# An RWKV scan on one core: the operands for the chunk ends dropped, and the order on the engines rewritten

## The reference, cut to the stage that is changed

The whole reference is three blocks; the change lies in the mixer below. `B` is 1, `L` is 512, and the 1024 channels are 16 heads of `N` = 64.

## Time and profile before

| | |
|---|---|
| time, median of three runs | 4066.91 us (4065.96 to 4070.18) |
| time of the profiled execution | 4058.67 us |
| its span, first to last instruction | 4057.3 us |
| stretch of the scan, first mask of the first half to first mask of the last | 1777.39 to 2128.79 us |
| in that stretch: TensorE, VectorE, ScalarE busy | 292.56, 286.25, 160.38 us of 351.40 |
| mean granted TensorE clock in it | 0.94 |

### The profile page before, as it was taken

One profiled execution on the slowest core, in us unless ns is written; L12 is line 12 of the kernel. 1 busy time (PEld: TensorE's weight loads), 2 busy tenths in 40 slices (PEclk: granted clock), 3 DMA queues, 4 the chain that ended last, 5 costly groups with the idle time before them and its releaser, 6 DMA issues. The chain is left out here.

```text
span 4057.3 us, 63395 instructions
## 1 busy us (share of the span) xinstructions
PE 3854.9 (95%) x26412; PEld 3044.2 (75%) x26412; DVE 2282.2 (56%) x3290; ACT 1318.3 (32%) x2121; POOL 1348.0 (33%) x550
## 2 busy tenths in 40 slices
PE   8999999999999999988888999999999999999998
PEld 6856788876778887577775788777777787877886
DVE  5746477567677665568884776465550626251033
ACT  3246233343223332444443433322222112103222
POOL 1001444443234441000001444355554343654442
PEclk9999999999999999999998999999999999999998
DMA  5310222232112223441112222222122112222221
GB/s 176 125 50 35 93 94 99 88 132 104 62 63 104 103 83 111 160 151 45 49 45 87 83 89 98 90 83 83 67 79 75 66 63 90 88 104 83 101 86 62
DMA packets 43375, 359.85 MB, mean 89 GB/s; under 512 B 4307, under 2 KB 4691, under 8 KB 23804
## 3 DMA queue, kind: packets, MB, share of 16 engines
q1 hardware_dynamic: 43132, 356.35, 24.3%
HBM read 333.79 MB, written 22.28 MB: 88 GB/s over the span
## 5 line engine op out<-in xcount | busy, mean ns | idle before, releaser
L352 POOL TENSOR_TENSOR ffn_weights_low<-weight_ring,ffn_weights_high 128x2048 fp32r<-128x2048 f32 x128 | 591.8, 4624 | 787.3 <-ACT ffn_weights_high L451 786.6
L202 PE MATMUL banks<-ffn_in_high,ffn_weights_low 128*128 128x512 f32 x2048 | 800.8, 391 | 12.8 <-POOL ffn_weights_low L352 8.8
L203 PE MATMUL banks<-ffn_in_low,ffn_weights_high 128*128 128x512 f32 x2048 | 798.2, 390 | 0.0
L204 PE MATMUL banks<-ffn_in_high,ffn_weights_high 128*128 128x512 f32 x2048 | 798.2, 390 | 0.0
L202 PEld LDWEIGHTS banks<-ffn_in_high,ffn_weights_low 128*128 128x128 f32 x2048 | 385.4, 188 | 98.9 <-POOL ffn_weights_low L352 11.3
L204 PEld LDWEIGHTS banks<-ffn_in_high,ffn_weights_high 128*128 128x128 f32 x2048 | 385.3, 188 | 80.6
L203 PEld LDWEIGHTS banks<-ffn_in_low,ffn_weights_high 128*128 128x128 f32 x2048 | 385.3, 188 | 80.0 <-issue 0.7
L451 ACT ACTIVATE ffn_weights_high<-weight_ring 128x2048 fp32r<-128x2048 f32 x128 | 245.2, 1915 | 560.0 <-PE banks L204 560.0
L605 DVE SCALAR_TENSOR_TENSOR ffn_gate<-ffn_up,columns_sb,ffn_gate 128x511 f32<-128x511 f32 (+1 forms) x132 | 273.6, 2072 | 160.8 <-ACT ffn_value L495 160.8
L3764 POOL TENSOR_TENSOR third_weights_low<-weight_ring,third_weights_high 128x1024 fp32r<-128x1024 f32 x144 | 359.8, 2498 | 11.5
L3762 POOL CAST third_weights_high<-weight_ring 128x1024 fp32r<-128x1024 f32 x144 | 159.4, 1107 | 512.4 <-PE banks L204 483.4
(11 more groups left out here) (646 smaller groups left out, 7474.4 us busy)
## 6 DMA issues: line engine op xcount, KB each, us to landing
weight_ring<-weights SPq DMA_DIRECT2D x144, 2048.0 KB, 7.7
scan_in<-rwkv_operands SPq DMA_DIRECT2D x7, 1280.0 KB, 5.8
rwkv_operands<-rwin_staged SPq DMA_DIRECT2D x23, 256.0 KB, 3.3
scan_in<-rwkv_operands SPq DMA_DIRECT2D x8, 512.0 KB, 3.9
bias_tiles<-bias_rows SPq DMA_DIRECT2D x8, 448.0 KB, 8.9
residual<-x SPq DMA_DIRECT2D x4, 512.0 KB, 7.1
hyena_u_x_T<-decay SPq DMA_DIRECT2D x2, 1024.0 KB, 8.0
rwkv_residual<-residual SPq DMA_DIRECT2D x1, 2048.0 KB, 7.2
```

The source lines that it names most:

```text
L202: pe.matmul(out, w[1], x[0], start=start, stop=False, skip_group_check=True)
L203: pe.matmul(out, w[0], x[1], start=False, stop=False, skip_group_check=True)
L204: return pe.matmul(out, w[0], x[0], start=False, stop=stop, skip_group_check=True)
L352: pool.tensor_tensor(parts[1], landed, parts[0].bitcast(F32), ALU.subtract).then_inc(S["split"], 1)
```

```diff
             def offsets(u):
...
-                for p in range(2):
-                    need(u, "phi_done", p + 1)
-                    act.activation(psi[:, p::2, :], B(d, 2 + p)[:, 256:512].rearrange("p (j k) -> p j k", j=JT), ACT.Copy)\
+                need(u, "sums_read", 1)
+                for c in (*order[d][1 - d::2], *order[d][d::2]):
+                    need(u, "phi_sum", 2)
+                    at = 256 + c // 2 * RW_N
+                    act.activation(psi[:, c, :], B(d, 2 + c % 2)[:, at:at + RW_N], ACT.Copy, scale=pe_end[:, u % 4, c:c + 1])\
                        .then_inc(S["psi_done"], 1)
...
-            def tails(u):
-                if not 0 <= u < HALVES:
-                    return
-                behind = upto(left) if u % 2 == FWD else ahead(grown)
-                dve.tensor_tensor(by_chunk(hat[:, 0, :]), by_chunk(k), behind, ALU.mult)
-                dve.tensor_tensor(by_chunk(hat[:, 1, :]), by_chunk(b), behind, ALU.mult).then_inc(S["tails_ready"], 1)
...
-                need(u, "diag_done", 1)
+                need(u, "psi_done", N_CHUNKS)
                 for p in range(2):
-                    need(u, "phi_sum", p + 1)
-                    dve.tensor_tensor(phi[:, p::2, :], B(d, 2 + p)[:, 0:256].rearrange("p (j k) -> p j k", j=JT), diag[:, d, p::2, :], ALU.add)\
+                    dve.tensor_tensor(phi[:, p::2, :], B(d, 2 + p)[:, 0:256].rearrange("p (j k) -> p j k", j=JT), spread(eye, JT), ALU.add)\
                        .then_inc(S["phi_done"], 1)
...
-                dve.tensor_tensor(state[:, d, n + 1, :], B(d, 3)[:, n * RW_N:(n + 1) * RW_N], psi[:, order[d][n], :], ALU.add)\
-                   .then_inc(S["state_done"], 1)
+                c = order[d][n]
+                dve.scalar_tensor_tensor(out=state[:, d, n + 1, :], in0=B(d, 3)[:, n * RW_N:(n + 1) * RW_N], scalar=pe_end[:, u % 4, c:c + 1],
+                                         in1=psi[:, c, :], op0=ALU.mult, op1=ALU.add).then_inc(S["state_done"], 1)
...
-                substituted(u, range(0, 2))
+                substituted(u, range(0, SUB - 1))
+                blocks_placed(u)
                 transitions(u - 1)
-                substituted(u, range(2, SUB - 1))
+                bonus_times_value(u)
                 state_step(u - 1, 1)
-                blocks_placed(u)
```

More of the change, by code:

```diff
@@ L2409, in rwkv_projection @@
                   "mixed_out", "gained_out", "key_in", "decays_in", "reset_in", "masks_in", "first_share", "first_key", "first_gain", "first_read",
-                  "scanned", "opened", "exponents", "inverse_exp", "exps", "prepared", *(f"staged_out_{m}" for m in range(KT)))
+                  "scanned", "opened", "inverse_exp", "exps", "prepared", *(f"staged_out_{m}" for m in range(KT)))
         sb = lambda name, shape, dt=F32: G.sb("rwin_" + name, shape, dt, ctx=ctx)
@@ L2813, in rwkv_scan @@
         NG = G.sb("scan_NG", [P, 2, 2, JT, 2, RW_CHUNK], ctx=ctx)
[L2814 to L2815 removed]
+        AR, KB, masks, bonus, pe_end = T.AR, T.KB, T.masks, T.bonus, T.pe_end
         phi = G.sb("scan_phi", [P, N_CHUNKS, RW_N], ctx=ctx)
@@ L3107, in _ @@
                 bonus_sums(u)
+                within(u - 1)
+                turned(u, 2)
                 state_step(u - 1, 1)
-                within(u - 1)
+                crossed(u, 3)
                 state_step(u - 1, 2)
-                turned(u, 2)
                 state_step(u - 1, 3)
-                crossed(u, 3)
+                carried(u, 3)
                 state_step(u - 1, 4)
-                carried(u, 3)
+                turned(u, 3)
                 state_step(u - 1, 5)
-                turned(u, 3)
+                crossed(u, 4)
                 state_step(u - 1, 6)
-                crossed(u, 4)
                 past(u - 1)
@@ L3440, in bonus_times_value @@
                    .then_inc(S["bonus_done"], 1)
-            for sem in ("keys_ready", "rows_ready", "sides_ready", "tails_ready", "bonus_in", "scanned", "exponents"):
+            for sem in ("keys_ready", "rows_ready", "sides_ready", "bonus_in", "scanned"):
                 dve.sem_inc(S[sem], 1)
@@ L3450, in _ @@
                 masked(u, 1)
-                substituted(u, range(0, 2))
+                substituted(u, range(0, SUB - 1))
+                blocks_placed(u)
                 transitions(u - 1)
-                substituted(u, range(2, SUB - 1))
+                bonus_times_value(u)
                 state_step(u - 1, 1)
-                blocks_placed(u)
+                bonus_product(u + 1)
+                written(u - 1)
+                crossed(u, 3)
                 state_step(u - 1, 2)
-                bonus_product(u + 1)
-                bonus_times_value(u)
-                written(u - 1)
+                read(u - 1)
                 state_step(u - 1, 3)
-                crossed(u, 3)
-                read(u - 1)
+                carried(u, 3)
                 state_step(u - 1, 4)
-                carried(u, 3)
+                keys(u + 1)
                 state_step(u - 1, 5)
+                crossed(u, 4)
                 state_step(u - 1, 6)
-                keys(u + 1)
-                crossed(u, 4)
                 sides(u + 1)
                 carried(u, 4)
+                past(u - 1)
                 rows_read(u + 1)
-                past(u - 1)
-                tails(u + 1)
                 crossed(u, 5)
@@ L3660, in rwkv @@
             T.KB = G.sb("scan_KB", [P, 2, SEQ], ctx=inner)
-            T.hat = G.sb("scan_hat", [P, 2, SEQ], ctx=inner)
+            G.sb("scan_spare", [P, 2, SEQ], ctx=inner)
             T.masks = G.sb("scan_masks_sb", [P, MASKS], ctx=inner)
```

67 lines of the change are left out of this document (23 added, 44 removed).

## The result

Each kernel ran five times: 4068.56 us before (4065.96 to 4071.62), **4095.71 us after** (4087.25 to 4101.13). The ratio is 1.0068, 95% interval 1.0057 to 1.0079: the change costs 27 us. The forecast was 4078, with a range to 4090. The two profiled executions are 37 us apart, since that of before was a short one: 31 of them lie in the scan, 6 in the rest of the launch.

What follows compares the result with a forecast made beforehand. The scan was taken as bound by waits between TensorE and VectorE. Over 15 halves, 10.2 (0.68 each) plus 1.8 (0.12 each) minus 1 gave +11 on the median 4066.91: 4078 us, own range 4072 to 4084, full range 4057 to 4090.

Steps and rivals of the forecast that it cites:

- The steps in the half: Scan: each step's new time followed through the shortest half found; `grams` ends at 1964.99 and the half ends 0.68 us later.
- The term of 0.80 us a half: Scan: 0.68 us a half from the level-4 end, plus 0.12 for two state steps on the path with column scalars.
- Psi: Ahead of phi: eight scaled copies on ScalarE take 2.00 us, bounds 0.67 and 2.7, ending before the placing is done.
- The column scalar: State steps: a scalar from a column adds 0.06 us each; two of six lie on the path, 0.12 a half.
- The reason I gave for 0.68: Level-4 mask: the sixth step stands behind it and `past` follows, so `carried` starts at 1961.23 instead of 1960.38.
- the walk that starts late: First state step, after phi behind the placing: the state is written 1.36 us later than before.
- The pauses: TensorE pauses in `within` can hide, since it ends about 1.2 us ahead of the placing: 1 us off the scan.
- more half clock: Rival, chance 0.13: thinner TensorE work in the scan lowers mean clock to 0.90, 28 us more slow, 9 lost: 4087.
- Cover for the pauses: Rival, chance 0.22: a third of 2.09 us a half in pauses and low clock hides, cancelling 0.68; 4062 to 4071.
- VectorE as the bound: Rival, chance 0.20: sixth step and `past` hide under other work, scan halves gain 0.43 to 1.13 us; 4050 to 4060.

Runs made afterwards that it cites:

- Sixth: Changed kernel with the sixth state step ahead of the level-4 `crossed` on TensorE and ahead of the level-4 mask on VectorE; 4105.46 us, ratio 1.0086 to before.
- past_behind: Changed kernel with `past` behind the level-4 `carried` on TensorE, nothing else moved; 4093.78 us, ratio 1.0077 to before.
- fill: Changed kernel with three unread matmuls a half (256, 128, 256 columns) where TensorE waits for the state; 4080.41 us, ratio 1.0039 to before.
- within_mid: Changed kernel with `within` behind the second state step on TensorE and its copy moved later on VectorE; 4129.85 us, ratio 1.0165 to before.
- fill_one: Changed kernel with one unread matmul of 256 columns a half, ahead of the third state step; 4084.04 us, ratio 1.0036 to before.

## Why the prediction was wrong

**The steps in the half were right at full clock, from the level-3 mask on.** Offsets from a half's start, forecast against the best half of after: placing 10.14 against 10.15; `phi` 10.74 against 10.81; level-3 mask 13.31 against 13.32; level-4 mask 16.58 to 17.00 against 16.87 to 17.29; `past` 17.40 against 17.74; `carried` 18.22 against 18.47; `grams` ended 21.98 against 22.26; the half 22.14 against 22.31. But that half is even and my sum was for an odd one, with other work between `phi` and the level-3 mask, so that the agreement there is in part luck. The one odd half without half clock, from 1903.67, has its first state step at 12.86 where I had 11.91 and its level-3 mask at 14.32 where I had 13.31, and is 23.31 us long. Behind the level-3 mask both take 8.99 us, where I had 8.71 and the best half of before 7.93. The term of 0.80 us a half (0.68 and two scalars) is 0.97 between best halves, and 0.4 between means freed of half clock, 6 us of the 12 forecast.

**Psi.** Between my bounds of 0.67 and 2.7, eight copies took 1.75 us; each is 0.35 us long, but they start 0.20 apart, so they overlap. I had them end before the placing was done, and in the best half they did; in seven of the 14 halves with a walk they came late and `phi` waited for them, 5.8 us in all:

```profile
  DVE scan_phi L3361: 5.8, 7
```

(From the list of who waited for line 3163 between 1777 and 2160, us and times.) My best half, in which nothing is late, could not show it, and it is part of the 0.4 us a half. By the Trainium skill's figures ("VectorE: DVE Perf Modes", the TRN2 errata, and "ScalarE: Activation LUTs") eight took 2.3 us by my estimate. The trace has 1.75, because they overlap by 0.15 us each. The Trainium skill ("ScalarE: Activation LUTs", the same section on `ACT_TABLE_LOAD` and timing) has an overlap of about 93 ns back to back, which my estimate left out.

**The column scalar.** A state step takes 0.28 against 0.22 us: the 0.06 was right.

**The reason I gave for 0.68 was half right.** I put it on the sixth step's place. Sixth and past_behind show that neither of two other places gives it back. What is left of my own sum is the line further up, the walk that starts late: 1.36 us by the forecast, 1.56 by the means of the first state step. That this is the cause at full clock is argued and not shown, since no run started the walk earlier.

**The pauses.** I took 1 us off because `within` would end 1.2 us ahead of the placing, so that a pause in it hides. It ends later than that. TensorE, then VectorE, in the odd half from 1903.67:

```profile
1914.83 0.28 PE L3032 MATMUL banks<-scan_MH,scan_UA 64*64 64x64 f32 x3 [1.94 <-issue]
...
1915.56 0.66 PE L2936 MATMUL banks<-constants_sb,scan_X 128*128 128x128 f32 x4
```

```profile
1913.80 0.69 DVE L3335 TENSOR_TENSOR scan_X<-scan_small,scan_masks_sb 128x512 f32<-128x512 f32 x1
...
1916.53 0.28 DVE L3392 SCALAR_TENSOR_TENSOR scan_state<-banks,scan_decay,scan_psi 128x64 f32<-128x64 f32 x1 [1.33 <-PE banks L3051]
```

A pause of 1.94 us inside `within` ends behind the placing, and `turned` and the first state step wait for it. In ten of the 14 halves `turned` starts 0.2 to 2.2 us later than the 10.88 at which it can, 0.8 us on average. All the same the level-3 mask comes 0.54 us earlier than before on average, where I had 0.09, and pauses fell from 21.6 to 18.0 us over the scan, those behind the level-3 mask from 0.33 us a half to none. So by these two traces the pauses cost some 4 us less and not 1, but not in the way I named.

**The step that failed** is the rival "more half clock": it was kept out of the sum, at a chance of 0.13 and a mean clock of 0.90, 28 us more at half clock and 9 us lost. Its mechanism and nearly its rate were right (a third lost by the `past` rows, 0.37 by the twin halves), but the clock was 0.86, 68 us more, some 25 us lost. It came on top of the waits at full clock, which cost 6 us where I had 12. With 68 x 0.37 = 25 in the sum the forecast would have been 4103, 7 us too much. I had seen that TensorE's work would thin out and priced it by a guess of 0.04 in the clock. Rows to size it better were there: the scan of before already had 42 us at half clock, in seven of its 14 halves with a walk and in the first, and a change that spreads single steps over the whole of the levels could touch most halves, at up to the 6.8 us that such a half of before showed. The Trainium skill ("TensorE: Matmul & The Clock Gate", Part 1), which ties the clock to how busy the array was, agrees with fill and within_mid. The Trainium skill ("TensorE: Matmul & The Clock Gate", Terms) also gives a price, the time at half rate x (1 - K/N), which is half of it; the twin halves lost 0.37.

**The other rivals.** Cover for the pauses came in part, as said, and was far too small to cancel the rest. VectorE as the bound falls: VectorE did 13.8 us less and waits for `grams`.

## What to carry to other kernels

When a change spreads small dependent steps between larger work, price TensorE's clock as a term of the sum and not as an unlikely case: count the halves that could fall, and take the rate from a pair of like stretches, one at each level. A late chain was not mended here by moving its last link; look for where it starts, and check in the trace that an edit meant to start it earlier does so, since an instruction can wait on another engine's queue. And put work into a hole only after asking which hole it leaves.

## What the runs showed of the hardware

- Unread matmuls, 42 in the scan (84 records of TensorE, busy for 28 us in all), made a kernel 12 to 15 us faster by holding the granted clock at 0.97 instead of 0.86.
- The same work can go either way: up to 14.50 us the twin halves had 12.45 and 12.37 us of TensorE, all at 1.00, and only in one the clock then fell. In fill_one ten of 15 halves have no half clock and three have 10.2 us.
- Scaled copies of 128x64 from PSUM on ScalarE take 0.35 us each, start 0.20 us apart, and take 1.75 us for eight.
- TensorE pauses, mostly inside a group of matmuls, with nothing in the profile that ends the pause: 21.6 us over the scan before and 18.0 after, the longest 1.94 us. What it waits for is not shown.
